# Moving 16 prompt tokens of a product-key layer from row fetches to dense products

## The chip, the cores and the metric

The kernel runs on one core of a Trainium2 chip. Its engines work beside one another and meet at semaphores: TensorE (PE in the profile), VectorE (DVE), ScalarE (ACT), GpSimd (POOL) and SyncE (SP), which issues most of the DMA transfers. The transfers of the core are carried by 16 DMA engines. The metric is the device time of one execution in microseconds (us), the median of several runs.

## The reference: what is computed

One decoder layer over 512 prompt tokens and 64 sample tokens (8 requests of 8), 2048 channels wide, all in float32: a modulated norm, a mixer with two kinds of heads, a residual; then a second modulated norm, the product-key retrieval ("PEER") that this change is about, a second residual and a final norm. The retrieval, per token and for each of 8 heads, picks 16 of 128 x 128 = 16384 experts, each one row of `peer_u` and one of `peer_v`:

```python
s1, i1 = lax.top_k(s[:, :, 0], PEER_TOPK)
s2, i2 = lax.top_k(s[:, :, 1], PEER_TOPK)
...
idx = jnp.take_along_axis(cidx, pos, axis=-1)
gates = jax.nn.softmax(top_s, axis=-1)
u_rows = p['peer_u'][idx]
act = jax.nn.gelu(jnp.einsum('phkd,pd->phk', u_rows, xb).astype(jnp.float32))
coef = (gates * act).astype(xb.dtype)
return jnp.einsum('phk,phkd->pd', coef, p['peer_v'][idx])
```

So a token needs 128 rows of `peer_u` and 128 rows of `peer_v`, 8 KB each. Both tables together hold 268 MB.

## The kernel before

The 576 tokens (T) lie along the free axis; the 2048 channels are 16 tiles of 128 partitions. For the retrieval they are parted in two.

**The dense tokens** (DT = 320: 256 prompt and 64 sample) are multiplied with all 16384 experts. The tables stream through once in "halves" of 128 x 1024 elements (512 KB): SP loads a half into `raw` (`load_half`, L233; four buffers in this stage, so a load waits until the half four before it has been split), ACT rounds it to `whi` (L244), POOL, or DVE for every fourth half, takes the rest `wlo` (L248, L253), and PE multiplies with three matmuls per tile (hi x hi, hi x lo, lo x hi), 24 matmuls of 320 columns for a half. A group is 4 x 128 experts: step A makes its `u` products (8 halves, L263), ACT applies gelu, DVE multiplies with the gates (L2195) and splits into `chi` and `clo`; step B makes the `v` products (8 halves, L2099) into two banks that DVE adds to `outacc` (L2228). There are 32 groups. The `u` products of the first two are made early, while DVE still selects the experts of the last head. Then 15 turns B, A, B, A follow (a turn is 32 halves, 768 matmuls), and two B at the end. The gates of a dense token, zero for nearly all experts, are built before that as outer products of one-hot rows (L1853 to L1902): 4 blocks of GB = 40 tokens to a loop turn, 8 tokens (an "octet") at a time, copied to `gst` and stored to `gateD` in HBM in pieces of 4 x 40 x 4 = 640 bytes, one store per block (L1831), two `gst` buffers.

**The sparse tokens** (SPT = 256, two row tiles of 128, one token on a partition) fetch only their own rows. `fetch` (L1801) is an indirect DMA of POOL: for one of the 128 slots it brings one row of 8 KB to each partition of a ring buffer, 1 MB. DVE takes a row set (`take`, L2162): for `u` a multiply and sum over 2048 elements, for `v` a multiply and add into PSUM. There are 512 fetches in this order: `u` of tile 0, `u` of tile 1, `v` of tile 0, `v` of tile 1, 128 each. The orders of POOL and DVE are written out in full for the whole stage: in the first eight turns 32 row sets fall to a turn (`rows_due`), in the seven later ones 35.4 on average, and 8 to the first B at the end. The ring has RING = 6 buffers; a fetch into one waits until DVE has taken what was in it. `xrow` holds the token rows of tile 1 until ACT copies them to PSUM between the two tiles of `u` (`between_rows`, L2142).

The query product (L1607, `parted`) multiplies with columns 0:256 and 256:576, one from each layout (`hi_s`, `hi_d`).

## Time and profile before

| | us |
|---|---|
| median of 3 runs | 4236.36 (4228.61 to 4244.34) |
| the profiled execution | 4242.22 |
| its span, first to last instruction | 4240.3 |

| engine | busy us | share of the span |
|---|---|---|
| PE | 3691.2 | 87% |
| DVE | 3024.4 | 71% |
| POOL | 2050.7 | 48% |
| ACT | 1471.0 | 35% |
| 16 DMA engines (mean) | 1090.68 MB moved | 257 GB/s over the span |

The program runs in stages. Modulation, mixer and output projection take the time up to about 1690 us, query and selection up to 2007 us with the early products in their last 65 us, the building of the gates 2007 to 2152 us. The stage of dense products and row sets runs from 2160 to 4216 us, nearly half of the span, and the final norm and output close it. A mean over the span mixes these: TensorE is the busiest engine on the page, while the DMA engines, with 257 GB/s on average, carry about 400 GB/s in the last stage. So the stage is read by itself, in stretches of one turn.

### The profile page before, as it was taken

What the parts mean: (1) busy time and instruction counts of PE and PEld (TensorE: products, weight loads), DVE (VectorE), ACT (ScalarE), POOL (GpSimd) and SP (SyncE); (2) the same over time, 40 slices, a digit from 0 to 9 for tenths busy, and PEclk for the clock granted to TensorE, in tenths of its full rate; (3) what the DMA queues carried; (4) which work ended last, traced back from release to release, by engine and by line L of the source; (5) the groups of instructions that cost most, each with busy time, mean ns of one, the idle gap of its engine ahead of it and who ended that gap; (6) DMA issues with size and microseconds to landing.
All of it is one profiled execution on the core that took longest, in us unless ns stands there. A gap on an engine that the chain in (4) does not pass through costs nothing. (4 is left out here: it accounts for less than half of the span.)

```text
span 4240.3 us, 66262 instructions
## 1 busy us (share of the span) xinstructions
PE 3691.2 (87%) x24298; PEld 3423.3 (81%) x24298; DVE 3024.4 (71%) x4791; ACT 1471.0 (35%) x1882; POOL 2050.7 (48%) x1144
## 2 busy tenths in 40 slices
PE   6876999999997898997679999999999898898986
PEld 3335988888896797997578888999898888888886
DVE  4777655566655214898978777778878888888886
ACT  5665444434442113222332332333332322223222
POOL 2333222222224233334047676777777767676772
PEclk9997999999998898998999999999999999999998
DMA  7991222222222123222589999999999999999994
GB/s 301 347 345 66 87 81 85 75 81 79 75 66 100 53 101 114 74 78 92 174 317 401 397 415 396 402 408 418 414 401 405 412 396 418 403 409 416 406 413 169
DMA packets 256208, 1090.68 MB, mean 257 GB/s; under 512 B 25352, under 2 KB 78856, under 8 KB 176392
## 3 DMA queue, kind: packets, MB, share of 16 engines
q1 hardware_dynamic: 170512, 543.60, 34.6%
q0 software_dynamic: 73728, 536.90, 30.9%
q10 hardware_dynamic: 11776, 7.52, 0.6%
q8 instruction: 132, 2.16, 0.2%
q14 instruction: 60, 0.49, 0.0%
HBM read 1047.54 MB, written 40.40 MB: 257 GB/s over the span
## 5 line engine op out<-in xcount | busy, mean ns | idle before, releaser
L248 POOL TENSOR_TENSOR wlo<-raw,whi 128x1024 fp32r<-128x1024 f32 x551 | 1344.4, 2443 | 1333.5 <-ACT whi L244 1328.2
L244 ACT CAST whi<-raw 128x1024 fp32r<-128x1024 f32 x670 | 699.1, 1049 | 1285.2 <-DMA raw<-in_u 535.1
L2099 PE MATMUL gps<-chi,whi 128*128 128x320 f32 x2048 | 656.7, 321 | 110.5 <-DVE outacc L2228 80.9
L263 PE MATMUL gps<-hi_d,whi 128*128 128x320 f32 x2048 | 653.2, 319 | 92.7 <-DVE wlo L253 61.9
L2099 PE MATMUL gps<-chi,wlo 128*128 128x320 f32 x2048 | 645.8, 315 | 0.0
L2099 PE MATMUL gps<-clo,whi 128*128 128x320 f32 x2048 | 645.7, 315 | 0.0
L263 PE MATMUL gps<-lo_d,whi 128*128 128x320 f32 x2048 | 643.6, 314 | 0.0
L263 PE MATMUL gps<-hi_d,wlo 128*128 128x320 f32 x2048 | 643.2, 314 | 0.0
L2186 DVE SCALAR_TENSOR_TENSOR dps<-ring,coef,dps 128x2048 f32<-128x2048 f32 x252 | 591.8, 2348 | 4.7 <-DVE dps L2186 0.9
L2173 DVE CUSTOM_DVE_ANT_0 ring<-ring,dps 128x2048 f32<-128x2048 f32 x256 | 582.2, 2279 | 0.0
L280 PE MATMUL gps<-act_hi,whi 128*128 128x288 f32 x2080 | 477.2, 311 | 37.9 <-POOL act_lo L511 9.0
L2099 PEld LDWEIGHTS gps<-chi,whi 128*128 128x128 f32 x2048 | 397.1, 194 | 130.9 <-DVE outacc L2228 92.8
L263 PEld LDWEIGHTS gps<-hi_d,whi 128*128 128x128 f32 x2048 | 394.4, 193 | 113.9 <-DVE wlo L253 69.8
L1807 POOL DMA_INDIRECT ring<-in_u_rows,spi x256 | 262.6, 1026 | 395.8 <-DVE udot L2173 224.9
L280 PE MATMUL gps<-act_hi,wlo 128*128 128x288 f32 x2080 | 450.1, 298 | 0.0
L280 PE MATMUL gps<-act_lo,whi 128*128 128x288 f32 x2080 | 448.4, 297 | 0.0
L2099 PEld LDWEIGHTS gps<-clo,whi 128*128 128x128 f32 x2048 | 397.2, 194 | 0.3
L2099 PEld LDWEIGHTS gps<-chi,wlo 128*128 128x128 f32 x2048 | 396.1, 193 | 0.0
L263 PEld LDWEIGHTS gps<-lo_d,whi 128*128 128x128 f32 x2048 | 394.4, 193 | 0.0
L263 PEld LDWEIGHTS gps<-hi_d,wlo 128*128 128x128 f32 x2048 | 394.4, 193 | 0.0
L280 PEld LDWEIGHTS gps<-act_hi,whi 128*128 128x128 f32 x2080 | 337.2, 192 | 63.5 <-issue 35.7
L280 PEld LDWEIGHTS gps<-act_hi,wlo 128*128 128x128 f32 x2080 | 338.3, 191 | 0.0
(384 smaller groups left out, 5906.6 us busy)
## 6 DMA issues: line engine op xcount, KB each, us to landing
raw<-in_u SPq DMA_DIRECT2D x256, 512.0 KB, 10.5
raw<-in_v SPq DMA_DIRECT2D x256, 512.0 KB, 8.6
wada<-in_w_ada SPq DMA_DIRECT2D x96, 1024.0 KB, 6.6
raw<-in_w_in SPq DMA_DIRECT2D x96, 512.0 KB, 3.4
gateD<-gst SPq DMA_DIRECT2D x8, 2560.0 KB, 9.9
gate<-gateD SPq DMA_DIRECT2D x32, 640.0 KB, 13.5
raw<-in_w_out SPq DMA_DIRECT2D x32, 512.0 KB, 3.7
raw<-in_w_q SPq DMA_DIRECT2D x32, 512.0 KB, 3.8
```

The source lines that it names most:

```text
L244: act.copy(whi[:, k.slot, :], raw_of(k)).then_inc(W.hi, 1)
L248: pool.tensor_tensor(wlo[:, k.slot, :], raw_of(k), whi[:, k.slot, :].bitcast(F32), ALU.subtract).then_inc(W.lo, 1)
L263: m = pe.matmul(gps[:, bank, 0:DT], w, x[:, kt, :], start=(kt == 0 and n == 0), stop=(kt == KT - 1 and n == 2))
L280: m = pe.matmul(gps[:, 2 * pair + th, 0:cols.stop - cols.start], w, parts[th][part][:, kt, cols], start=(kt == 0 and n == 0), stop=(kt == ...
L1807: pool.indirect_dma_start(out=rings[row_slot[n]][:, :], out_offset=None, in_=src, in_offset=bass.IndirectOffsetOnAxis(ap=spi[:, tile % NST ...
L2099: m = pe.matmul(gps[:, 2 + dt, 0:DT], w[:, slot, cols], x[:, buf, c, :], start=(c == 0 and n == 0), stop=(c == NG - 1 and n == 2))
L2173: m = dve.tensor_tensor_reduce(out=got, in0=got, in1=rows4, scale=1.0, scalar=0.0, op0=ALU.mult, op1=ALU.add, accum_out=udot[:, tile, j:j ...
L2186: m = dve.scalar_tensor_tensor(got if j == NSLOT - 1 else rows4, got, by, rows4, ALU.mult, ALU.add)
```

## The change

The split moves from 256 and 320 tokens to 240 and 336. The first row tile keeps 128 tokens, the second has 112: its fetches, multiplies and final transposes use partitions 0 to 111. All dense products of the retrieval have 336 columns. The gates are built in 3 loop turns of 4 blocks of 28 tokens in place of 2 turns of 4 blocks of 40: 42 octets and 12 stores in pieces of 4 x 28 x 4 = 448 bytes. The sparse layout `hi_s` stays 256 columns wide, so tokens 240 to 255 stand in both layouts and the query product still multiplies 256 and 320 columns. The larger dense buffers leave no room for the sixth ring buffer: its place is taken by `xrow`, which is free only after ACT has copied it, so the ring has five buffers up to row set 132 and six from 133. `udot` is cleared once, since tile 1 no longer fills all partitions.

```diff
-SPT = 256
-NST = SPT // P
+SPT = 240
+NST = 2
+SW = NST * P
+SROWS = (P, SPT - P)
 DT = T - SPT
-GB = 40
+GB = 28
...
-        hi_s, lo_s = (sb(n, [P, KT, SPT], F32R, at=at2nd) for n in ("hi_s", "lo_s"))
+        hi_s, lo_s = (sb(n, [P, KT, SW], F32R, at=at2nd) for n in ("hi_s", "lo_s"))
...
-        parted = [(hi_s, lo_s, slice(0, SPT)), (hi_d, lo_d, slice(0, DT))]
+        parted = [(hi_s, lo_s, slice(0, SW)), (hi_d, lo_d, slice(SW - SPT, DT))]
...
+        XROW_FROM = NSLOT + RING - 1
...
-                free[0:0] = range(RING0, RING)
+                free[0:0] = range(RING0, RING - 1)
+            if n == XROW_FROM:
+                free[0:0] = [RING - 1]
...
+            elif n == XROW_FROM:
+                pool.wait_ge(xrow_free, 1)
             tile, j = n // NSLOT, n % NSLOT
             src = a["u_rows"] if tile < NST else a["v_rows"]
+            used = slice(0, SROWS[tile % NST])
             pool.indirect_dma_start(
-                out=rings[row_slot[n]][:, :], out_offset=None, in_=src,
-                in_offset=bass.IndirectOffsetOnAxis(ap=spi[:, tile % NST, j:j + 1], axis=0)
+                out=rings[row_slot[n]][used, :], out_offset=None, in_=src,
+                in_offset=bass.IndirectOffsetOnAxis(ap=spi[used, tile % NST, j:j + 1], axis=0)
             ).then_inc(w_row[row_slot[n]], 16)
...
-        rings += [sb(f"ring{n}", [P, D], at=at7) for n in range(RING0, RING)]
+        rings += [sb(f"ring{n}", [P, D], at=at7) for n in range(RING0, RING - 1)] + [xrow]
...
-                    fetched, due = [RING0], [RING0 - RING]
+                    fetched, due = [RING0], [RING0 + 1 - RING]
...
-                        if n < min(due[0] + RING - (LAG if n >= NSP // 2 else 0), NSP):
-                            fetch(pool, n, S.taken)
+                        if n < min(due[0] + RING - (n < XROW_FROM) - (LAG if n >= NSP // 2 else 0), NSP):
+                            fetch(pool, n, S.taken, S.xt)
...
+                    ch(dve.memset(udot[:, :, :], 0.0))
```

On POOL, where tile 0 of the `u` rows gives way to tile 1 (the number in a ring's name is its buffer; `raw_11280` and `raw_10635` are the same load buffer). Before:

```order
352 L1807 DMA ring_8956<-in_u_rows,spi 128x2048
353 L248 TENSOR_TENSOR wlo<-raw_11280,whi 128x1024
354 L1807 DMA ring_8957<-in_u_rows,spi 128x2048
355 L248 TENSOR_TENSOR wlo<-raw,whi 128x1024
356 L1807 DMA ring_8958<-in_u_rows,spi 128x2048
357 L1807 DMA ring_8959<-in_u_rows,spi 128x2048
358 L248 TENSOR_TENSOR wlo<-raw_11280,whi 128x1024
359 L1807 DMA ring_11281<-in_u_rows,spi 128x2048
360 L248 TENSOR_TENSOR wlo<-raw_11280,whi 128x1024
361 L1807 DMA ring_11282<-in_u_rows,spi 128x2048
```

The same place on POOL after the change:

```order
355 L1816 DMA ring_8958<-in_u_rows,spi 128x2048
356 L1816 DMA ring_8959<-in_u_rows,spi 112x2048
357 L251 TENSOR_TENSOR wlo<-raw_10635,whi 128x1024
358 L1816 DMA ring_10636<-in_u_rows,spi 112x2048
359 L251 TENSOR_TENSOR wlo<-raw_10635,whi 128x1024
360 L1816 DMA ring_8956<-in_u_rows,spi 112x2048
361 L251 TENSOR_TENSOR wlo<-raw,whi 128x1024
362 L1816 DMA ring_8957<-in_u_rows,spi 112x2048
363 L1816 DMA ring_8958<-in_u_rows,spi 112x2048
364 L251 TENSOR_TENSOR wlo<-raw_10635,whi 128x1024
365 L1816 DMA xrow<-in_u_rows,spi 112x2048
```

A fetch stands at the same point between the `wlo` of the halves; it is one row set less ahead, it brings 112 rows from tile 1 on, and the first one into `xrow` has a `wlo` between it and the fetch before.

On DVE, at the end of a step A and the start of a step B around the first take of tile 1. Before (each take is the row with a ring in it and the short one behind it):

```order
1645 L2173 ISA ring_11282,udot<-ring_11282,dps 128x2048
1646 L2173 ISA udot 128x1
1647 L2200 TENSOR_TENSOR clo<-gps,chi 128x320
1648 L253 TENSOR_TENSOR wlo<-raw,whi 128x1024
1649 L2228 TENSOR_TENSOR outacc<-outacc,gps 128x320 x2
1650 L2173 ISA ring_8956,udot<-ring_8956,dps 128x2048
```

After:

```order
1640 L2185 ISA ring_8958,udot<-ring_8958,dps 128x2048
1641 L2185 ISA udot 128x1
1642 L2212 TENSOR_TENSOR clo<-gps,chi 128x336
1643 L256 TENSOR_TENSOR wlo<-raw,whi 128x1024
1644 L2240 TENSOR_TENSOR outacc<-outacc,gps 128x336 x2
1645 L2185 ISA ring_8959,udot<-ring_8959,dps 112x2048
```

Nothing changes places on DVE; the dense instructions are 16 elements longer, and a take of tile 1 has 112 partitions and the same 2048 elements on each.

## Rows read from the trace of the kernel before

**Rows 1.** The page: the GB/s of 40 slices, and two DMA issues.

```profile
GB/s 301 347 345 66 87 81 85 75 81 79 75 66 100 53 101 114 74 78 92 174 317 401 397 415 396 402 408 418 414 401 405 412 396 418 403 409 416 406 413 169
...
gateD<-gst SPq DMA_DIRECT2D x8, 2560.0 KB, 9.9
```

**Rows 2.** Windows of one turn each: stretch, length, busy us per engine, clock, DMA share, GB/s.

```profile
core 0: us, PE busy (x) PEld busy (x) DVE busy (x) ACT busy (x) POOL busy (x), PEclk, DMA share, GB/s
2160.20:2289.15 128.95, 117.78 (x769) 114.42 (x769) 102.52 (x128) 42.50 (x53) 91.31 (x56) 0.98 1.01 405
2289.15:2419.29 130.14, 119.22 (x768) 116.83 (x769) 100.34 (x120) 40.79 (x49) 89.71 (x56) 0.96 0.99 399
...
2802.44:2926.46 124.02, 115.74 (x769) 112.63 (x769) 100.33 (x120) 39.82 (x48) 91.05 (x56) 1.00 1.01 413
2926.46:3051.13 124.67, 116.05 (x770) 112.67 (x769) 100.34 (x120) 39.82 (x48) 90.94 (x56) 1.00 1.02 414
...
3718.07:3851.53 133.46, 119.07 (x771) 116.89 (x769) 114.84 (x92) 39.69 (x48) 94.25 (x60) 0.96 1.01 410
3851.53:3985.21 133.68, 120.67 (x770) 119.09 (x769) 115.26 (x92) 39.37 (x48) 95.20 (x60) 0.94 1.00 407
3985.21:4121.12 135.91, 119.60 (x770) 117.24 (x769) 114.95 (x92) 39.38 (x48) 94.82 (x60) 0.96 1.01 414
```

**Rows 3.** DMA view, 2700 to 3180 us: row queue (packets, MB, share), two issues.

```profile
q0 software_dynamic: 17493, 127.43, 64.6%
...
raw<-in_v SPq DMA_DIRECT2D x61, 512.0 KB, 8.4
...
ring<-in_u_rows,spi POOLq DMA_INDIRECT x117, 9.0
```

**Rows 4.** What PE waited for, 2300 to 4100 us: total, times, longest.

```profile
PE gps L2099 <- DVE outacc L2228: 74.7, 58, 3.7
PE gps L263 <- DVE wlo L253: 55.5, 27, 3.7
PE gps L263 <- POOL wlo L248: 27.5, 29, 2.9
PE gps L2099 <- DVE clo L2200: 3.9, 1, 3.9
```

**Rows 5.** What ACT waited for, the same stretch.

```profile
ACT whi L244 <- DMA raw<-in_u: 480.7, 163, 7.5
ACT whi L244 <- DMA raw<-in_v: 331.5, 132, 8.7
```

**Rows 6.** The DMA view of 1931 to 1938 us: loads with little beside them.

```profile
raw<-in_u SPq DMA_DIRECT2D x2, 512.0 KB, 3.4
```

**Rows 7.** Timeline of PE, from 1759.8 us (columns 320 and 256).

```profile
1759.83 0.31 PE L280 MATMUL gps<-lo_d,whi 128*128 128x320 f32 x1
1759.98 0.28 PE L280 MATMUL gps<-hi_s,wlo 128*128 128x256 f32 x1
1760.10 0.31 PE L280 MATMUL gps<-hi_d,wlo 128*128 128x320 f32 x1
```

**Rows 8.** Timeline of PE in a step B: start, duration.

```profile
2871.74 0.31 PE L2099 MATMUL gps<-chi,whi 128*128 128x320 f32 x1
...
2872.77 0.31 PE L2099 MATMUL gps<-clo,whi 128*128 128x320 f32 x1
```

**Rows 9.** Timeline of DVE in the building of the gates: two octets.

```profile
2126.66 1.21 DVE L1878 TENSOR_TENSOR gb<-pairT,const 128x1024 f32<-128x1024 f32 x1
...
2129.84 1.21 DVE L1878 TENSOR_TENSOR gb<-pairT,const 128x1024 f32<-128x1024 f32 x1
```

**Rows 10.** DMA view, 2031 to 2041 us: one gate store (pieces of 640 bytes).

```profile
q1 hardware_dynamic: 4112, 2.62, 85.0%
```

**Rows 11.** DMA view, 469 to 476 us: a store in pieces of 432 bytes.

```profile
q10 hardware_dynamic: 144, 0.06, 3.0%
```

**Rows 12.** DMA view, 401 to 404 us: a store from 8 partitions, 9216 bytes each.

```profile
q1 hardware_dynamic: 16, 0.07, 20.9%
...
rowsD<-rowT SPq DMA_DIRECT2D x1, 72.0 KB
```

**Rows 13.** DMA view, 4228.5 to 4239.5 us: stores of the output from 128 partitions.

```profile
q1 hardware_dynamic: 1025, 4.13, 94.0%
```

**Rows 14.** The row fetches (L1807): time from issue to landing.

```profile
DMA to landing us min/median/max: 5.4/9.4/14.1
```

**Rows 15.** Timeline of ACT: the copy of `xrow` between the tiles.

```profile
2678.32 1.87 ACT L2142 COPY dps<-xrow 128x2048 f32<-128x2048 f32 x1 [1.77 <-DVE udot L2173]
```

More of the change, by code:

```diff
@@ L1376, in build @@
         X.saved, = sems(stack, "x_saved")
-        at4 = [after]
+        at4 = [after2]
         x1T = sb("x1T", [P, KT, T], at=at4)
@@ L1497, in build @@
         EARLY = 2
-        at5 = [after]
+        at5 = [after2]
         clo = sb("clo", [P, EARLY, NG, DT], F32R, at=at5)
-        early = sb("early", [P, EARLY, NG, DT], at=[after])
+        early = sb("early", [P, EARLY, NG, DT], at=[after2])
         spi = sb("spi", [P, NST, H * TOPK], U32, at=at5)
@@ L1656, in body @@
                                 act.wait_ge(S.score, h * 2 + (s - 1))
-                            ch(act.copy(qt[:, s, 0:SPT], gps[:, 2 * s, 0:SPT]))
-                            act.copy(qt[:, s, SPT:T], gps[:, 2 * s + 1, 0:DT]).then_inc(S.qev, 1)
+                            ch(act.copy(qt[:, s, 0:SW], gps[:, 2 * s, 0:SW]))
+                            act.copy(qt[:, s, SW:T], gps[:, 2 * s + 1, 0:T - SW]).then_inc(S.qev, 1)
                             if s == 0 and later:
@@ L1799, in build, with fetch @@
             used_last[slot] = n
-        def fetch(pool, n, taken):
+        def fetch(pool, n, taken, xrow_free=None):
             if row_before[n] is not None:
                 pool.wait_ge(taken, row_before[n] + 1)
+            elif n == XROW_FROM:
+                pool.wait_ge(xrow_free, 1)
             tile, j = n // NSLOT, n % NSLOT
             src = a["u_rows"] if tile < NST else a["v_rows"]
+            used = slice(0, SROWS[tile % NST])
             pool.indirect_dma_start(
-                out=rings[row_slot[n]][:, :], out_offset=None, in_=src,
-                in_offset=bass.IndirectOffsetOnAxis(ap=spi[:, tile % NST, j:j + 1], axis=0)
+                out=rings[row_slot[n]][used, :], out_offset=None, in_=src,
+                in_offset=bass.IndirectOffsetOnAxis(ap=spi[used, tile % NST, j:j + 1], axis=0)
             ).then_inc(w_row[row_slot[n]], 16)
@@ L1839, in _ @@
                     for k in range(3):
-                        for t in range(NCH - NST):
-                            pe.transpose(gps[:, k, t * CH:(t + 1) * CH], slots[:, NST + t, k, :], ident)
+                        for t in range(NCH - NST + 1):
+                            pe.transpose(gps[:, k, t * CH:(t + 1) * CH], slots[:, NST - 1 + t, k, :], ident)
                         m = pe.transpose(gps[:, 3, k * TS:(k + 1) * TS], slots[0:TS, NCH, k, :], const[0:TS, 0:TS])
@@ L1862, in _ @@
                     for k in range(3):
-                        act.copy(slotT[k][:, 0:DT - TS], gps[:, k, 0:DT - TS]).then_inc(S.trev, 1)
+                        act.copy(slotT[k][:, 0:DT - TS], gps[:, k, SROWS[1]:SROWS[1] + DT - TS]).then_inc(S.trev, 1)
                         act.copy(slotT[k][:, DT - TS:DT], gps[:, 3, k * TS:(k + 1) * TS]).then_inc(S.trev, 1)
@@ L2058, in B @@
                             next_row()
-                    for _ in range(RING - RING0):
+                    for _ in range(RING - 1 - RING0):
                         next_row()
@@ L2072, in from_rows @@
                             for t in range(NST):
[L2073 to L2075 removed]
+                                o, n_ = (k % 8) * SW + t * P, SROWS[t]
+                                m = pe.transpose(rows4[:, o:o + n_],
+                                                 rings[row_slot[(LAST0, NSP - 1)[t]]][0:n_, k * P:(k + 1) * P],
+                                                 ident[0:n_, 0:n_])
                         m.then_inc(S.tr, 1)
@@ L2167, in take @@
                         tile, j = n // NSLOT, n % NSLOT
-                        got = rings[row_slot[n]][:, :]
+                        used = slice(0, SROWS[tile % NST])
+                        got, acc = rings[row_slot[n]][used, :], rows4[used, :]
                         dve.wait_ge(w_row[row_slot[n]], 16 * row_turn[n])
@@ L2172, in take @@
                                 dve.wait_ge(S.xt, tile)
-                            m = dve.tensor_tensor_reduce(out=got, in0=got, in1=rows4, scale=1.0, scalar=0.0,
+                            m = dve.tensor_tensor_reduce(out=got, in0=got, in1=acc, scale=1.0, scalar=0.0,
                                                          op0=ALU.mult, op1=ALU.add,
-                                                         accum_out=udot[:, tile, j:j + 1])
+                                                         accum_out=udot[used, tile, j:j + 1])
                         else:
```

14 lines of the change are left out of this document (6 added, 8 removed).

## The prediction, made before the changed kernel ran

> **What bounds the kernel now.** I read the GB/s line of the page first: over the last half of the span it stands at about 400, over the middle below 120 [rows 1]. The change acts mostly there, so I took windows of one turn (32 halves, 768 matmuls) [rows 2]. Three things are to be seen. The DMA share is 0.99 to 1.02 in every turn: the 16 engines are never idle. PE is busy 116 to 121 us of 124 to 136, and 13 of those us are only the modelled ends: eight consecutive starts take 1.03 us, 147 ns each [rows 8], so 768 matmuls need 112.9 us. And the turn's length follows the row sets: 32 of them in the first eight turns, 124.0 to 130.1 us; 35.4 in the later ones, 133.5 to 135.9 us in the rows shown, with the same matmuls in both.
>
> In bytes: a turn loads 32 x 0.524 = 16.8 MB of halves, 4 x 0.655 = 2.6 MB of gates and 32 x 1.049 = 33.6 MB of rows, 53.0 MB, later 56.5 MB. The ratio is 1.067; 134.4 us (mean of the three later turns) over 127 us (about the mean of the first eight, of which two ends are shown) is 1.06. That is a stage bound by DMA. The waits agree: ACT waits 812 us for halves to land, 480.7 + 331.5 [rows 5]; a half takes 8.4 us from issue to landing there [rows 3] and 3.4 us with little beside it [rows 6]. PE waits 162 us of 1800, for `outacc`, `wlo` and `clo` [rows 4], which come late because of that or because DVE is inside a take. DVE never waits for a row set: its ring is full in time.
>
> **Outside that stage** there is no DMA to hide behind. (1) Early products: 8 x 48 = 384 matmuls, back to back. Sixteen columns more cost 16/320 of 147 ns, 7.3 ns; the step from 256 to 320 columns (0.12 to 0.14 us between starts [rows 7]) gives 5 to 7 ns. I take 7: +2.7 us. (2) Gates: DVE makes an octet in 3.18 us (2126.66 to 2129.84 [rows 9]) and sets the pace; two more octets are +6.4 us. The stage ends when the last store has landed, now 9.9 us [rows 1]. A store keeps 4112 packets; a 640-byte one takes 0.85 x 10 us x 16 / 4112 = 33 ns [rows 10], a 432-byte one 0.03 x 7 x 16 / 144 = 23 ns [rows 11]. At 25 ns the last store lands about 2 us earlier: -2 us. The other stores end beside the building: a block of 28 tokens takes 3.5 x 3.18 = 11.1 us. (3) The two B at the end: 384 matmuls, +2.7 us. (4) 16 columns more in the second modulation and one memset: +0.5 us. Sum: **+10.3 us**.
>
> **The turns, PE side.** 768 x 7.3 ns = 5.6 us of PE per turn, 84 us over 15 turns. While DMA sets the turn this lies in PE's idle time: 127 - 112.9 = 14 us early, 134.4 - 112.9 = 21 us later, less what the half clock takes (clock 0.94 to 1.00). It isn't free: PE has less room after a late half. The bounds are 0 and 5.6 us a turn. I take 1 us, nearer to nothing, because the later turns took 3.5 MB more at the same rate, 407 to 414 GB/s, with PE at a different load: **+15 us**. DVE's 752 dense instructions get 16 elements longer, about 17 ns by 482 ns for 320 and its fixed part: 12 us in all, in the same shade.
>
> **The turns, DMA side.** Tile 1's 256 fetches bring 112 rows: 33.6 MB less. The row queue spends 0.646 x 480 x 16 = 4961 engine-us on 127.43 MB [rows 3], 319 ns for a row of 8 KB with its share of the small packets, so a fetch holds each of 16 engines for 8 x 319 ns = 2.55 us. Spread evenly, 112 rows would hold them 7 x 319 ns: 0.32 us less, 82 us over 256 fetches. That is one bound. The other is above nothing, and here I chose against the bytes. The trace has one transfer that doesn't cover 128 partitions and is large enough to read: the store of `rowT` from 8 partitions. Its 8 packets of 9216 bytes take 0.209 x 3 us x 16 = 10.0 engine-us, 1.25 us each [rows 12], 7.4 GB/s per engine. Stores from 128 partitions run at 4.13 MB / (0.94 x 11 us x 16) = 25 GB/s [rows 13]. So an engine's rate depends on which partitions the transfer touches: neighbours share something that 128 partitions use evenly. In a fetch of partitions 0 to 111 the sixteen missing rows are neighbours too. If they lie on a few of these shared ways, the others carry as much as before, and the fetch holds the transfers as long as one of 128 rows. I take that: **0 us** for tile 1's bytes, the value between the bounds that the nearest row speaks for.
>
> The Trainium skill, page "SBUF — State Buffer", section "Door 1: The DMA port swizzle", says this in full: 16 ports of 8 partitions, by bits of the partition number, about 27 GB/s each. By it partitions 112 to 127 share four ports with 80 to 95, so twelve ports keep their eight rows a fetch; the sum stays at 0 for this term, where bytes alone would give -82 us before PE's floor. The trace agrees in the one place it can: four neighbours on one port would be a quarter of the rate, and 7.4 of 25 is 0.30.
>
> **Ring and new wait.** With five buffers a fetch is issued at least four takes ahead, 4 x 3.9 us = 15.6 us, and lands in 9.4, at most 14.1 us [rows 14]: hidden, at about 0. The fetch into `xrow` waits on POOL for ACT's copy of 1.87 us, which starts when tile 0's last `u` row is taken [rows 15]. Queued behind it are POOL's `wlo` halves, for which PE waits. But the fetch before it waits for the same take and a `wlo` of 2.4 us stands between: 0, at worst 2 us, once.
>
> **Sum.** 10.3 + 15 + 0 = +25 us. Against the profiled execution 4242.2 + 25 = 4267; against the median, 6 us below it, 4236 + 26: **4262 us**, 0.6% slower.
>
> **Rivals.**
> A. *Bytes count evenly; faster or no change.* For it: DMA is the bound, and 4.2 MB of 53.0 go in a tile-1 turn. Against: rows 12. The gain stops at the next floor. Early tile-1 turns: DMA 125 x 48.9/53.0 = 115 us, PE 118.5 us plus about 3.5 for the change of step where DVE is late, so 123.5 in place of 125: -1.5 x 4. Later ones: DMA 124 us, DVE 116 + 1, PE 118.5 + 3.5 + 3 for the clock, so 128 in place of 134.4: -6.4 x 3.6 = -23. Tile 0 keeps +1 x 7.6. Total 10.3 + 7.6 - 29 = -11: 4225 us, 4200 to 4245. It decides when a tile-1 row packet stays near 319 ns.
> B. *The 112 rows get in one another's way; slower.* If the even split gives an engine seven rows that lie on other engines' ways, packets slow down. 8/7 x 319 = 365 ns is the point at which nothing is saved; at 400 ns a fetch costs 7 x 35 = 0.25 us more, +63 us over 256. With the 25: 4325 us. The far end, 1.25 us as in rows 12, would be over 1000 us; I don't hold the range to it, since there only 8 partitions were in use. For it: the same rows. Against: in 112 rows the neighbours need not coincide.
> C. *PE becomes the bound everywhere*: 5.6 x 15 + 10.3 = +94, 4330 us. For it: the half clock in some turns. Against: the idle time above.
> D. *Pieces of 448 bytes are slow.* The Trainium skill, page "DMA: Bandwidth & Descriptors", section "Specifications", wants at least 512 bytes and names a read-modify-write below. From rows: were a packet twice the 33 ns, a store would take 17 us against 11.1 us of building, and 12 of them 204 us in place of 140: +64 and the 25, 4325 us. The 23 ns of rows 11 speak against it.
>
> **How the numbers follow.** Forecast 0.40, A 0.30, B 0.23, C 0.04, D 0.03. The forecast's own range is 4245 to 4280. The range for 8 in 10 runs from inside A, 4210, to inside B, 4345. The measurement tells about 0.5% (21 us) from no change. Faster by more: a quarter of A, 0.08. Within: most of A, 0.20, 0.17 of the forecast and 0.02 of B, 0.39. Slower: the rest, 0.53.
>
> **What the changed profile would show.** PE starts 154 ns apart, and no PE wait in the early products. Gates: 42 octets, stores landing in about 8 us; 13 or more means D. Turns of tile 0: 1 us longer, DMA share still 1.0. Turns of tile 1: the same length as before with fewer GB/s (about 380 in place of 410) if I am right; share below 1 and turns of 124 and 128 us for A; row packets over 365 ns and longer turns for B. A DVE wait for a ring buffer would make the five-buffer step wrong; a `wlo` wait beside the first fetch into `xrow`, the new wait. The forecast is wrong if DMA isn't the bound of tile 0's turns, or if tile 1's lose length.

## The result: 9.8% slower

| | before | after |
|---|---|---|
| median of 4 runs, us | 4237.92 | 4659.50 (4618.67 to 4684.12) |
| ratio, 95% interval | 1 | 1.0982 [1.0940, 1.1023] |
| the profiled execution, us | 4242.22 | 4676.66 |
| its span, us | 4240.3 | 4674.7 |

The forecast was 4262, its range 4210 to 4345: the time lies 315 us above the range. The GB/s line of the page after, beside [rows 1], shows where. The 40 slices are now 117 us each.

```profile
GB/s 302 354 272 74 85 76 82 77 69 82 65 85 82 101 95 74 75 168 268 386 382 405 379 246 275 299 282 281 280 401 404 400 413 298 265 261 258 249 262 152
...
L2198 DVE SCALAR_TENSOR_TENSOR dps<-ring,coef,dps 128x2048 f32<-128x2048 f32 (+1 forms) x205 | 481.8, 2350 | 77.8 <-DMA ring<-in_v_rows,spi 75.0
...
gateD<-gst SPq DMA_DIRECT2D x12, 1792.0 KB, 8.8
```

Twice the rate falls from about 400 to 250 to 300 GB/s, in six slices and then in six more: these are tile 1 of `u` and tile 1 of `v`, the two quarters whose fetches bring 112 rows. Between them stands tile 0 of `v`, with 128 rows a fetch, at 400 and more. And DVE waits 75.0 us for row sets of `v`, which it never did before.

The windows of one turn each, as in [rows 2] (stretch, length, busy us of PE, PEld, DVE, ACT, POOL, clock, DMA share, GB/s). The first two are of tile 0 of `u`, then two of tile 1 of `u`, one of tile 0 of `v`, two of tile 1 of `v`:

```profile
2166.42:2297.76 131.34, 122.94 (x769) 120.68 (x769) 103.68 (x128) 43.87 (x54) 88.38 (x56) 0.98 0.98 392
2297.76:2431.90 134.14, 123.35 (x769) 120.74 (x769) 101.19 (x121) 39.01 (x47) 88.73 (x57) 0.97 0.97 385
...
2697.49:2882.79 185.30, 136.74 (x771) 131.53 (x769) 104.31 (x120) 41.24 (x49) 89.73 (x58) 0.88 1.02 259
2882.79:3051.13 168.34, 134.04 (x770) 130.56 (x769) 104.12 (x120) 40.22 (x49) 89.06 (x56) 0.89 1.02 292
...
3388.97:3525.65 136.68, 125.10 (x770) 122.87 (x769) 116.98 (x93) 39.55 (x49) 94.94 (x60) 0.96 1.00 403
...
4139.60:4335.88 196.28, 138.08 (x769) 131.99 (x769) 114.47 (x92) 39.65 (x48) 91.74 (x60) 0.87 1.01 257
4335.88:4535.32 199.44, 137.45 (x768) 131.64 (x769) 113.84 (x93) 39.65 (x48) 91.06 (x59) 0.86 1.01 256
```

A turn of tile 1 takes 166 to 199 us in place of 124 to 136, with fewer bytes, the DMA share still at 1.01 or 1.02 and the busy time of DVE, ACT and POOL little changed. The granted clock falls to 0.86 to 0.91, a mean of 1.2 and 2.4 GHz: in 2880 to 3060 us there are seven stretches of 3.4 to 10.2 us at the lower level, each soon after PE had stood idle for 1.8 to 8.7 us. So the DMA engines are full and move less. The DMA view tells why (queue: packets, MB, share of the 16 engines; then issues with KB and median us to landing). First 2700 to 3380 us, tile 1 of `u`:

```profile
q0 software_dynamic: 16170, 115.88, 63.9%
...
raw<-in_u SPq DMA_DIRECT2D x64, 512.0 KB, 16.8
...
ring<-in_u_rows,spi POOLq DMA_INDIRECT x103, 13.9
```

Then 3950 to 4550 us, tile 1 of `v`:

```profile
q0 software_dynamic: 14015, 100.44, 66.2%
...
raw<-in_u SPq DMA_DIRECT2D x48, 512.0 KB, 21.1
...
ring<-in_v_rows,spi POOLq DMA_INDIRECT x87, 19.5
```

The working of [rows 3]: 0.639 x 680 x 16 = 6952 engine-us for 115.88 MB is 491 ns for a row of 8 KB; in the second stretch it is 518 ns. Before it was 319. A load of `in_u` lands after 16.8 and 21.1 us, before after 11.0 and 10.1 (2700 to 3180 and 3500 to 4100 us). In the recorded packets the row packets of tile 1 have a mean of 486 (`u`) and 513 ns (`v`), in tile 0 325 and 318; the packets of the loads beside them (4 KB) 232 and 245 ns in place of 163 to 167.

What waited in 3900 to 4580 us (us in total, times, longest):

```profile
POOL wlo L251 <- ACT whi L247: 302.9, 73, 14.7
ACT whi L247 <- DMA raw<-in_u: 243.6, 44, 12.1
ACT whi L247 <- DMA raw<-in_v: 231.7, 53, 5.7
DVE gps L2207 <- ACT gps L2131: 111.9, 22, 11.4
...
PE gps L266 <- POOL wlo L251: 83.4, 20, 10.4
```

A late half is late for ACT, then for POOL's `wlo`, then for PE. ACT's longest wait for a load is 12.1 us, before it was 8.7 [rows 5]; PE's longest is 10.4 us, before it was 3.9 [rows 4].

### The profile page after: what moved, and what is told of

Its sections match the earlier page's. It is cut to its first block and busy times, and to the rows that moved or that the text cites. A ratio compares the mean times of both kernels' runs of the same rounds, so it can differ in the third digit from the quotient of the medians.

```text
span 4674.7 us, 66414 instructions
## 1 busy us (share of the span) xinstructions
PE 3872.3 (83%) x24333; PEld 3592.8 (77%) x24333; DVE 3055.5 (65%) x4810; ACT 1473.8 (32%) x1886; POOL 2019.2 (43%) x1144
## 5 line engine op out<-in xcount | busy, mean ns | idle before, releaser
L2109 PE MATMUL gps<-chi,whi 128*128 128x336 f32 x2048 | 692.1, 338 | 227.3 <-DVE outacc L2240 147.8
L266 PE MATMUL gps<-hi_d,whi 128*128 128x336 f32 x2048 | 680.5, 332 | 232.8 <-POOL wlo L251 156.7
L2109 PE MATMUL gps<-clo,whi 128*128 128x336 f32 x2048 | 677.4, 331 | 7.1 <-issue 7.1
L2109 PE MATMUL gps<-chi,wlo 128*128 128x336 f32 x2048 | 677.4, 331 | 0.0
L266 PE MATMUL gps<-lo_d,whi 128*128 128x336 f32 x2048 | 668.6, 326 | 0.0
L266 PE MATMUL gps<-hi_d,wlo 128*128 128x336 f32 x2048 | 667.9, 326 | 0.0
L2185 DVE CUSTOM_DVE_ANT_0 ring<-ring,dps 128x2048 f32<-128x2048 f32 (+1 forms) x235 | 534.8, 2280 | 0.0
L2198 DVE SCALAR_TENSOR_TENSOR dps<-ring,coef,dps 128x2048 f32<-128x2048 f32 (+1 forms) x205 | 481.8, 2350 | 77.8 <-DMA ring<-in_v_rows,spi 75.0
L1816 POOL DMA_INDIRECT ring<-in_u_rows,spi x235 | 225.2, 958 | 342.8 <-DVE udot L2185 168.5
L2240 DVE TENSOR_TENSOR outacc<-outacc,gps 128x336 f32<-128x336 f32 x512 | 251.7, 500 | 178.9 <-PE gps L2109 177.7
## 6 DMA issues: line engine op xcount, KB each, us to landing
gate<-gateD SPq DMA_DIRECT2D x32, 672.0 KB, 16.8
```

The source lines that it names most:

```text
L266: m = pe.matmul(gps[:, bank, 0:DT], w, x[:, kt, :], start=(kt == 0 and n == 0), stop=(kt == KT - 1 and n == 2))
L1816: pool.indirect_dma_start(out=rings[row_slot[n]][used, :], out_offset=None, in_=src, in_offset=bass.IndirectOffsetOnAxis(ap=spi[used, tile ...
L2109: m = pe.matmul(gps[:, 2 + dt, 0:DT], w[:, slot, cols], x[:, buf, c, :], start=(c == 0 and n == 0), stop=(c == NG - 1 and n == 2))
L2185: m = dve.tensor_tensor_reduce(out=got, in0=got, in1=acc, scale=1.0, scalar=0.0, op0=ALU.mult, op1=ALU.add, accum_out=udot[used, tile, j:j ...
L2198: m = dve.scalar_tensor_tensor(got if j == NSLOT - 1 else acc, got, by, acc, ALU.mult, ALU.add)
L2240: dve.tensor_tensor(out, out, gps[:, 2 + dt, 0:DT], ALU.add).then_inc(S.acc, 1)
```

## The experiments

All kernels are compared with the kernel before on the same chip. Where the time went is read by turns: the sum of the turns of each quarter, from the windows of the profiled executions, in us (the twelfth turn, in the third column, already has some row sets of tile 1 of `v`).

```
kernel           stage starts   u tile 0 u tile 1 v tile 0 v tile 1  rest    span
                                (4)      (4)      (4)      (3)
before                2160.2    514.9    500.2    542.8    403.0    119.2  4240.3
after                 2166.4    531.1    691.5    559.4    586.9    139.4  4674.7
before_fetch112       2160.1    513.6    704.0    549.6    583.8    145.5  4656.6
after_fetch128        2164.6    536.6    537.4    546.4    411.5    119.2  4315.8
skip_last16           2163.8    512.9    501.9    534.0    401.8    119.2  4233.6
skip_every8           2157.4    514.6    501.5    541.8    403.0    118.8  4237.0
before_ring5          2153.7    516.5    519.3    538.6    403.4    118.9  4250.5
ring5_catchup         2159.2    519.1    501.4    534.6    400.4    118.4  4233.0
cols336               2159.8    517.3    508.2    544.1    402.7    120.5  4252.6
ring5_cols336         2157.6    523.6    530.0    535.7    405.8    119.4  4272.1
after128_cols320      2160.7    526.1    517.7    535.5    402.7    118.4  4261.1
gates_once            2158.9    498.9    486.6    534.1    396.6    118.3  4193.5
after_skip_every8     2160.7    531.6    537.5    545.8    412.0    118.8  4306.4
before_cols304        2161.0    513.6    503.6    530.0    402.5    118.1  4228.8
before_lag0           2159.0    516.0    500.2    539.7    501.3    116.7  4332.8
before_lag1           2163.6    515.6    500.2    531.0    397.4    121.4  4229.1
before_lag01          2157.6    518.2    501.1    525.3    399.5    121.6  4223.3
```

Each line is one execution, and the quarters that an edit doesn't touch show how far they wander: tile 0 of `u` between 512.9 and 518.2, tile 1 of `u` within 1 us of 500.2, tile 0 of `v` from 534.0 to 542.8. Smaller differences in one column say nothing.

### The shape of the fetch, in the kernel

The theory after the result: a fetch of 112 partitions slows the packets of the rows and of all that runs beside them. The rival: the loss comes from the ring, the longer products or how they act together. The kernel before, with nothing changed but the 112 rows in tile 1 (its last 16 tokens get no rows, and their token rows are zero):

```diff
+            used = slice(0, 112 if tile % NST else P)
-                out=rings[row_slot[n]][:, :], out_offset=None, in_=src,
-                in_offset=bass.IndirectOffsetOnAxis(ap=spi[:, tile % NST, j:j + 1], axis=0)
+                out=rings[row_slot[n]][used, :], out_offset=None, in_=src,
+                in_offset=bass.IndirectOffsetOnAxis(ap=spi[used, tile % NST, j:j + 1], axis=0)
```

> The kernel before with one edit: tile 1's fetches bring 112 rows (16 tokens are left out: their token rows are zeroed, the instruction counts and sizes of all engines stay). Theory P: tile 1's turns lengthen by 45 and 60 us as in the changed kernel, about 4237 + 390 = 4630 us. Rival Q: 4237 or less.

And the changed kernel with 128 rows in tile 1 again (`used = slice(0, P)`):

> The changed kernel, but tile 1 fetches all 128 rows again (DVE still uses 112 of them). Theory P: the row packets return to 320 ns, tile 1's turns to about 130 and 136 us, and what is left over the kernel before is the 336 columns, the gates and the five-buffer ring: 4265 to 4285 us. Rival Q (336 columns, 112-partition DVE work or the ring cause the loss): it stays within 100 us of 4660.

before_fetch112: 4653.06 us (two runs), ratio 1.0969 [1.0936, 1.1001]. after_fetch128: 4318.91 us, 1.0179 [1.0157, 1.0202], 34 us above the range expected for it. The 112 rows make nearly the whole loss by themselves, 416 us, and giving the 16 rows back to the changed kernel wins 341. The two parts, 416 and 82, are more than the 422 together; that fits DMA as the bound of tile 1, beside which the other part has room again, but no run shows it by itself. One turn of tile 1 of `u` in each, in this order:

```profile
2855.08:3030.72 175.64, 132.10 (x769) 126.49 (x769) 101.15 (x120) 39.76 (x48) 87.06 (x56) 0.88 1.02 273
```

```profile
2965.42:3102.00 136.58, 126.31 (x770) 124.67 (x769) 106.41 (x120) 39.72 (x48) 91.67 (x57) 0.95 0.95 378
```

### The shape alone

A kernel of nothing but transfers: sections of 20 fetches of 8 KB rows to 128, 120, 112, 96 and 64 partitions, then with 20 loads of 512 KB beside them, then 40 loads alone. Nothing of the layer is computed, the outputs are zeros.

```diff
+                            pool.indirect_dma_start(
+                                out=rings[slot][0:width, :], out_offset=None, in_=a["u_rows"],
+                                in_offset=bass.IndirectOffsetOnAxis(ap=idx[0:width, n % NIDX:n % NIDX + 1], axis=0)
+                            ).then_inc(s_row[slot], 16)
```

> A kernel that computes nothing of the layer (its outputs are zeros): sections of 20 row fetches each, up to five in flight, to partitions 0:128, 0:120, 0:112, 0:96 and 0:64 alone, then 20 fetches of 128, 112 and 96 partitions beside 20 loads of 512 KB, then 40 loads alone. Theory P (neighbouring partitions share a way into SBUF, and a fetch of fewer than 128 rows sends several engines down the same way): 128 rows run at about 26 GB/s per engine (320 ns a row), 112 rows alone have packets clearly over 365 ns, so a fetch of 112 takes longer than one of 128, 96 as well, and 64 rows (half of the ways) about as long as 128. Beside loads, 112-row fetches stretch the loads' 4 KB packets from 160 to over 220 ns too. Rival Q (the slow packets come from this kernel's other traffic or timing, not from the shape of the fetch): 112 rows alone take 7/8 of the time of 128, at about 320 ns a row.

A single run, 732 us. Its windows by section (stretch, length, POOL busy, clock, DMA share, GB/s): 128, 120, 112, 96, 64 partitions, then 128 with loads, 112 with loads, and loads alone:

```profile
2.92:57.32 54.40, 18.89 (x20) 1.00 0.94 386
58.26:150.87 92.61, 19.45 (x20) 1.00 0.97 212
151.77:219.96 68.19, 18.30 (x20) 1.00 0.97 269
220.85:287.73 66.88, 18.07 (x20) 1.00 0.96 235
288.62:341.59 52.97, 17.85 (x20) 1.00 0.96 198
341.67:419.48 77.81, 18.69 (x20) 1.00 0.99 404
419.73:519.44 99.71, 18.35 (x20) 1.00 0.99 289
...
619.63:674.88 55.25, 0.00 (x0) 1.00 0.97 380
```

Share x length x 16 over the rows gives per row packet 320 ns for 128 partitions, 599 for 120, 472 for 112, 535 for 96 and 636 for 64. So 112 rows take 68.2 us where 128 take 54.4, and no width in between is cheaper than 128; 120 is the worst. With the loads, the mix of the kernel's turn, a pair of fetch and load takes 4.99 us in place of 3.89. A turn of 32 pairs is then 160 us, and 124.5 with 128 rows: the kernel has 166 to 185, and 124 to 127. The shape alone makes most of the loss, with no engine computing. It isn't POOL's share of the work either: a fetch holds POOL for 0.9 to 1.0 us at every width (18.89 / 20 for 128 partitions, 18.30 / 20 for 112).

Two more readings bear on how the rows are dealt to the engines. In the prediction's picture twelve engines keep eight rows and four have four, so that the share could reach at most (12 x 8 + 4 x 4) / 128 = 0.88 of full; it is 0.97 with 112 partitions, so the work is spread over all 16. And the DMA view counts 320 packets of 4 bytes beside the rows of 20 fetches, 16 a fetch, at every width but 120: there it counts 480, 24 a fetch, so the worst width is cut up in another way.

The Trainium skill, page "SBUF — State Buffer", section "Door 1: The DMA port swizzle", says that 64 partitions reach half of the ports and about half of the rate; 198 against 386 GB/s agrees. One way to it is rival B's: 16 engines carry a fetch, and if 112 rows are dealt out seven to an engine in order, one engine's rows lie on several of those ports and several engines meet at one. Which rows an engine carries no record here shows, so this is argued, not shown.

### Fewer bytes in the old shape

If that is so, a fetch that keeps 128 partitions but skips 16 rows, leaving each engine on its own way, must not slow down. The rival says that any missing row upsets it. The index of the skipped partitions is put out of bounds, and the 16 tokens are left out: partitions 112 to 127 in skip_last16, every eighth one (7, 15, ...) in skip_every8.

```diff
+                    ch(dve.tensor_scalar(slots[:, 1, 0, :], slots[:, 1, 0, :], const[:, C_SKIP:C_SKIP + 1], None, ALU.add))
+            more = dict(bounds_check=NKEY * NKEY - 1, oob_is_err=False) if tile % NST else {}
-                in_offset=bass.IndirectOffsetOnAxis(ap=spi[:, tile % NST, j:j + 1], axis=0)
+                in_offset=bass.IndirectOffsetOnAxis(ap=spi[:, tile % NST, j:j + 1], axis=0), **more
```

> The kernel before; tile 1's fetches keep all 128 partitions, but the indices of partitions 112 to 127 lie beyond the table's bound, so their rows are skipped (these 16 tokens are left out). The same bytes as with 112 rows. Theory P with the engines kept on their own ways: no packets slow down; the ways of the other rows carry as much as before, so 4230 to 4245 us, unchanged. If bytes were all that counts: 4200 or less. If skipping rows as such is slow: over 4300.

> The kernel before; tile 1's fetches keep 128 partitions but skip the rows of partitions 7, 15, ... 127 (16 tokens left out), so each group of neighbours loses one row in eight. The same bytes as skip_last16 and as 112 rows. Theory P with DMA as the bound of tile 1's turns: the whole saving is open, 0.32 us a fetch, 82 us at most; PE and DVE stop it: 4237 - 15 to - 45, so 4190 to 4222 us. If the stage is held equally by something else (PE's own idle time, DVE): within 10 us of 4237, as skip_last16.

The same in the changed kernel:

> The changed kernel with 128-partition fetches in tile 1 that skip every eighth row: 336 dense columns, the saved bytes taken evenly from all ways (other tokens left out than the kernel needs, the sizes are those of the change). It is what the change would have been had bytes counted evenly. Theory C (with 336 columns PE, not DMA, holds the early turns; after_fetch128 showed a DMA share of 0.95): little comes of it, 4290 to 4315 us. Rival A of the prediction (DMA is still the bound): 4225 to 4250 us.

skip_last16: 4240.35, 0.9998 [0.9983, 1.0012]. skip_every8: 4240.72, 1.0008 [0.9995, 1.0021]. after_skip_every8: 4313.95, 1.0178 [1.0156, 1.0199], the same as after_fetch128. A turn of tile 1 of `u` in skip_last16 and in skip_every8:

```profile
2801.59:2925.74 124.15, 116.98 (x768) 112.64 (x769) 101.15 (x121) 40.08 (x48) 95.84 (x56) 1.00 0.98 382
```

```profile
2798.05:2922.27 124.22, 117.33 (x768) 112.67 (x769) 101.16 (x121) 40.09 (x48) 95.86 (x56) 1.00 0.99 381
```

Row packets stay at 320 to 323 ns, so the shape and not the number of rows is the cause. skip_last16 says more: it brings the same rows to the same partitions, 0 to 111, as before_fetch112, and is 413 us faster. What differs is the width that the instruction states, and with it how the rows are dealt out.

The second finding was expected of skip_last16 and not of skip_every8, where 4190 to 4222 was the range if DMA is the bound: some 31 GB/s less, and the turn keeps its length within 0.2 us (124.02 in [rows 2]). In skip_last16 loads even land after 8.6 us in place of 11.1 (median of the `u` halves, 2700 to 3150 us). Fewer row bytes, taken in this way, win nothing.

But the edit takes away less than its bytes. In 2700 to 3150 us the row queue's share falls from 0.651 to 0.578 and 0.582, while the plain loads need 0.393 and 0.403 for the 65 MB that took 0.362; about half of the saving is gone. And a fetch with the bounds check holds POOL for 1.17 us in place of 1.01, 5 us more in a turn. So these two runs are not DMA alone made lighter.

### What else holds the turn

Three runs take something else away or add to it. 16 columns less in the dense products (the last 16 dense tokens get no products):

```diff
-                                gemm_dense(pe, k.plus(2 * c + half), half, c % 2)
+                                gemm_dense(pe, k.plus(2 * c + half), half, c % 2, DT - 16)
```

> The kernel before with 16 columns fewer, 304, in all dense matmuls of the last stage (the last 16 sample tokens' products are left out; DVE and ACT work on 320 as before). PE needs 15 x 768 x 7.5 ns = 86 us less. If DMA alone holds the turns: 4225 to 4240 us. If PE's columns count in full on the path: 4150 us. Theory C says PE and DMA are nearly level in the kernel before, so down to DMA's floor only: about 4215 to 4235 us.

16 columns more in 15 of 16 matmuls of A and 3 of 4 of B (`DT + 16` there; these columns hold neighbours' data, and their products are used by nothing):

> The kernel before; the matmuls of the last stage take 16 more columns (the neighbours' first columns, into bank columns that nobody reads), except those of the last tile of a product, so about 0.84 of the change's extra PE time, 5 us a turn; everything else as before. The step lengths so far: a step B holds DVE 0.93 to 0.98 busy and went from 30.6 to 33.3 us in after_fetch128, a step A stayed. Theory C: steps B lengthen by 1.5 to 2.5 us, A by under 0.5: 4237 + 40 to 65 us. The prediction's term (PE's columns lie in idle time, 1 us a turn): 4237 + 8 to 20.

And the gates of the first two groups used by all, with 30 loads of gates left out:

```diff
-                            if j == 0:
-                                load_gates(g, buf)
-                        dve.wait_ge(s_gate[g % 2], g // 2 * 16 + 16)
+                        dve.wait_ge(s_gate[g % 2], 16)
```

> The kernel before without the 30 later gate loads (all groups use the gates of the first two; 20 MB less). Steps A take 32 to 33.7 us where PE needs 28.1; skipping row bytes left them as they were. Theory G (a step A is held by the halves queued behind the gate load on SP's queue): steps A lose 1.5 to 3 us each, 4237 - 45 to - 90. If A is held by DVE and POOL: within 15 us of 4237.

before_cols304: 4229.09, 0.9973 [0.9963, 0.9982]: 11 us won for 86 us of PE, a time that lies in two of the three expected ranges. cols336: 4246.76, 1.0017 [0.9999, 1.0035]: 8 us lost for 71 us, not clear of the noise, and as the prediction's term has it. gates_once, a little less than the 45 us expected: 4197.23, 0.9904 [0.9884, 0.9923]. A turn of tile 1 of `u` there:

```profile
2900.68:3022.02 121.34, 115.36 (x769) 112.65 (x769) 100.32 (x120) 40.27 (x48) 91.02 (x56) 1.00 1.02 415
```

30 loads of 640 KB, 20 MB or 2.5% of the stage's bytes, bring 41 us, 2% of the stage's time, while 256 x 16 rows, 34 MB or 4%, bring nothing. ACT's longest wait for a `u` half in 2700 to 3150 us falls from 6.8 to 2.7 us (in the skip runs it stays at 7.2 and 7.4), and the steps A, from first matmul to first matmul, shrink from 33.7 to 31.5 us (tile 0) and 32.0 to 30.3 (tile 1), the steps B not at all. So a step A is held by its load of gates. Whether by the halves that queue behind it or by the bytes as such is open: in tile 1 of `u` a step A moves 13.2 MB in 32.0 us with the gates and 12.6 in 30.3 without, 414 and 416 GB/s, which is what a bound by DMA would give, and for the steps A only the skip runs speak against it.

A step B of tile 1 of `u` takes 30.55 us on average in the kernel before, with the DMA at 387 or at 418 GB/s, and as long in gates_once; in skip_last16 and skip_every8 it is 30.8. With 16 columns less it takes 29.7 and with the columns of cols336 31.2; with DVE's slow `wlo` of before_ring5, below, 32.7 (means of eight steps). DVE is busy 27.4 us of it, 0.90, not the 0.93 to 0.98 of the expectation for cols336. So DVE and PE hold a step B together. Two such steps of the kernel before, in the order of the windows above:

```profile
2675.06:2705.58 30.52, 28.84 (x193) 28.26 (x193) 27.39 (x36) 10.88 (x11) 23.12 (x15) 1.00 0.99 387
2864.23:2894.77 30.54, 28.78 (x193) 28.25 (x193) 27.41 (x36) 9.27 (x10) 22.48 (x15) 1.00 1.02 418
```

In before_cols304 the steps A of tile 1 give back what the steps B win, 33.3 us in place of 32.0. The turn has several limits of nearly the same length: taking away from one brings little.

### The ring of five

The kernel before with five buffers up to row set 132 and then six, its columns and fetches as they were:

```diff
-                free[0:0] = range(RING0, RING)
+                free[0:0] = range(RING0, RING - 1)
+            if n == FULL_FROM:
+                free[0:0] = [RING - 1]
-                        if n < min(due[0] + RING - (LAG if n >= NSP // 2 else 0), NSP):
+                        if n < min(due[0] + RING - (n < FULL_FROM) - (LAG if n >= NSP // 2 else 0), NSP):
```

> The kernel before with five ring buffers up to row set 132 and six after it, nothing else. after_fetch128 is 82 us over the kernel before, and its tile-0 turns are 5 us longer. Theory C (the columns do it): 4237 within 8 us. Rival R (fetches come later, or POOL's waits move against the wlo halves): 4250 to 4280 us.

With one extra fetch at set 133, so that from there on the fetches are six ahead again:

```diff
+                            if n == FULL_FROM:
+                                fetch(pool, n + 1, S.taken)
+                                fetched[0] += 1
```

> before_ring5 with one fetch more at the point where the sixth buffer becomes free, so that from there on POOL is again six ahead and waits for DVE's latest take. Its loss of 14 us lies in the turns of tile 1 of u, where DVE's wlo rose from 1.22 us. Theory L (POOL out of step with DVE): those turns return from 129.8 to 125 us, 4237 within 6 us. Otherwise it stays at 4250 to 4256.

before_ring5: 4253.48, 1.0033 [1.0021, 1.0045]. ring5_catchup: 4241.41, 1.0009 [0.9994, 1.0023]. The 14 us lie in tile 1 of `u` (500.2 to 519.3), where the ring has six buffers again; in tile 0, with five, a turn is as before. No row set is late. The order keeps fetching five ahead there, one buffer is mostly free, and POOL no longer waits for DVE's take before each fetch. DVE's `wlo` in 2802 to 3175 us (count | busy us, mean ns | idle), before and then in before_ring5 and ring5_catchup:

```profile
L253 DVE TENSOR_TENSOR wlo<-raw,whi 128x1024 fp32r<-128x1024 f32 x24 | 29.4, 1225 | 0.0
```

```profile
L253 DVE TENSOR_TENSOR wlo<-raw,whi 128x1024 fp32r<-128x1024 f32 x24 | 44.3, 1844 | 0.0
```

```profile
L253 DVE TENSOR_TENSOR wlo<-raw,whi 128x1024 fp32r<-128x1024 f32 x24 | 29.4, 1224 | 0.0
```

The mean of the same instruction is 1.84 us in place of 1.22, and one more fetch undoes it. The mean hides two kinds: in before_ring5 12 of the 24 take 1.22 us and 12 take 2.42 to 2.61. Each of the slow ones starts while a `wlo` of POOL is running and ends 1.1 us after that one's end; none of the quick ones overlaps it by more than 0.31 us. One of each kind, with POOL's instruction above (start, duration):

```profile
2932.79 2.37 POOL L248 TENSOR_TENSOR wlo<-raw,whi 128x1024 fp32r<-128x1024 f32 x1 [2.44 <-ACT whi L244]
2933.66 2.59 DVE L253 TENSOR_TENSOR wlo<-raw,whi 128x1024 fp32r<-128x1024 f32 x1
...
2949.70 1.22 DVE L253 TENSOR_TENSOR wlo<-raw,whi 128x1024 fp32r<-128x1024 f32 x1
```

While POOL waits at each fetch, its own `wlo` fall at fixed points between DVE's; let loose, they meet. The Trainium skill, page "SBUF — State Buffer", section "Who interferes with whom", says that a DVE instruction with two SBUF inputs, as this one, contends with a GpSimd instruction that reads SBUF; the 2.42 to 2.61 us agree.

Then the kernel before has the same loss in its `v` half: LAG = 2 there makes it fetch four ahead with six buffers, five in the last quarter. LAG = 0 and LAG = 1 for the whole half, and, third, 0 for tile 0 and 1 for tile 1, so that the lead equals the buffers in both:

```diff
-                        if n < min(due[0] + RING - (LAG if n >= NSP // 2 else 0), NSP):
+                        if n < min(due[0] + RING - (LAG - 1 if n >= 3 * NSP // 4 else 0), NSP):
```

> The kernel before with LAG = 0 in place of 2: in the v half of the stage POOL issues a fetch as soon as DVE has freed the buffer, as in the u half, and so runs in step with DVE. Theory L (DVE's wlo takes 1.86 us there and 1.22 us in the u half because POOL's own work runs across it; POOL in step with DVE avoids that): the wlo returns to 1.22 us, turns 8 to 14 lose 2 to 5 us each, 4205 to 4225 us. Otherwise: POOL's waits delay its own wlo halves and the turns lengthen, 4240 to 4280 us.

> LAG = 1: between the two. Theory L: DVE's wlo between 1.22 and 1.86 us in turns 8 to 14, 4220 to 4235 us.

> The kernel before with LAG 0 for tile 0 of v (where before_lag0 took a turn from 134.6 to 130.6 us) and 1 for tile 1 of v, where the ring has lost the buffer that keeps tile 0's sum and LAG 0 made POOL wait (167 us a turn). Theory L: 4217 to 4227 us, below before_lag1's 4231.

before_lag0: 4340.04, 1.0242 [1.0215, 1.0270], far above both ranges expected; its turns of tile 0 of `v` take 130 to 131 us in place of 133 to 137, but those of tile 1, where the order is one ahead of the ring's five buffers, 163 to 172: POOL waits 165.0 us for DVE's takes in 3720 to 4100 us (51.6 before), and its `wlo` stand behind these fetches. before_lag1: 4230.60, 0.9970 [0.9959, 0.9981]. before_lag01: **4220.19, 0.9958 [0.9942, 0.9975]**, with all of the work in it, some 0.4% under the kernel before. A turn of tile 0 of `v` before and in before_lag01:

```profile
3309.25:3446.31 137.06, 120.22 (x770) 117.83 (x769) 115.15 (x91) 39.05 (x48) 95.36 (x60) 0.95 1.01 409
```

```profile
3307.34:3436.71 129.37, 116.29 (x770) 112.62 (x769) 108.97 (x91) 39.92 (x48) 93.81 (x59) 1.00 1.02 418
```

DVE's `wlo` in 3200 to 3650 us, in the same order:

```profile
L253 DVE TENSOR_TENSOR wlo<-raw,whi 128x1024 fp32r<-128x1024 f32 x26 | 49.7, 1911 | 0.0
```

```profile
L253 DVE TENSOR_TENSOR wlo<-raw,whi 128x1024 fp32r<-128x1024 f32 x27 | 34.3, 1269 | 0.0
```

### What remains in after_fetch128

It is 1.8% slower than before, some 80 us. Alone, ring (14) and columns (8 for 0.84 of them) make 22. Both together in the kernel before (the edits of before_ring5 and cols336):

> The kernel before with both edits that alone gave +14 us (five buffers up to row set 132) and +8 us (336 columns in most matmuls). after_fetch128 is +80, of which these and the longer gates explain some 28. Theory I (the two together cost more than one by one, because in steps B PE and DVE are level and each edit uses the other's room): 4237 + 40 to 70 us, steps B of the u half 33 us. Theory D (the rest comes from the longer DVE and ACT instructions): 4237 + 20 to 28.

And after_fetch128 with 320 columns in the dense products, all else of the change kept:

> after_fetch128 with the last stage's matmuls back at 320 columns (16 sample tokens' products left out); DVE and ACT still work on 336, the ring and the gates as in the change. PE needs 90 us less. Theory I: the interaction goes with the columns, 4255 to 4275 us, steps B of the u half back at 30.8 us. Theory D: 4290 to 4310 us.

ring5_cols336: 4274.17, 1.0083 [1.0066, 1.0101], 35 us, between the two ranges expected. after128_cols320: 4266.65, 1.0074 [1.0057, 1.0091], 31 us, inside the range of theory I; but its steps B take 32.3 and 32.6 us in the two tiles of `u` and not 30.8, so that theory's reason did not come out. By the ratios, the same columns cost 8 us alone, 21 beside the five-buffer ring, and some 45 on top of all the rest (1.0179 against 1.0074, with all of them). The parts don't add. Of the 31 us, 14 are the ring's; the table has what is left mostly in tile 0 of `u`, 526.1 us in place of 516.5 in before_ring5. What in "all the rest" makes it there (longer DVE and ACT instructions, larger loads of gates), and why columns weigh so much on top of it, was not taken apart and stays open.

## Why the prediction was wrong

**The step that failed is "The turns, DMA side".** It went from "an engine's rate depends on which partitions the transfer touches" to "the others carry as much as before", and took 0 us for the bytes of tile 1. The first half is right: with 64 partitions the rate is 198 GB/s, with 128 it is 386. The second assumed that 112 rows keep each engine on the way that it has with 128; that holds when 128 partitions are stated and 16 rows skipped, and not when 112 are stated. Rival B named the other case and its mechanism stands: row packets above 365 ns. Its size did not hold. The text put 400 ns, from no row, and said that the far end, 1.25 us [rows 12], was not to be held. Measured were 486 and 513 ns: 7 x (486 - 365) = 0.85 us a fetch of `u` and 7 x (513 - 365) = 1.04 of `v`, 241 us over 2 x 128. The second part was in no case at all: the loads beside the fetches slow down too, by 8 x (232 - 166) = 0.53 and 8 x (245 - 166) = 0.63 us a half, about 141 us over the 7.6 turns. Together 382 us; the table, from `u` tile 1 to the end, has 363 between after_fetch128 and after. The same sum with the packets of before_fetch112 (493 and 236 ns, 517 and 251) gives 401, where 416 were measured.

**"A stage bound by DMA" was not shown by what it rested on, and stays undecided for the kernel before.** The share of 1.0 and turns that grow with the row sets fit it, but a row set also costs 2.35 us of DVE, and so grows the turn without DMA. The steps B, equally long at 387 and at 418 GB/s, and the skip runs speak against it, the steps A of gates_once for it. In the changed kernel with 128 rows the share is 0.95, so there DMA isn't the bound of these turns; with the slow packets it is. Two readings under it were off: a turn loads gates twice and not four times (7 loads in 2700 to 3180 us), so it moves 51.7 MB and not 53.0, later 55.2, which leaves the ratio at 1.07. And of PE's 116 to 121 us not 13 but 3 to 8 are modelled ends, by the text's own 112.9.

**Rival A** (4225, chance 0.30) falls by its own condition, packets near 319 ns. In after_skip_every8, where an eighth fewer rows come at 329 ns a packet, the time is 4314, as in after_fetch128: even with quick packets no gain was there.

**The ring, "hidden, at about 0", was 14 us.** The lead of 15.6 us was enough: no row set came late. What was missed is that the length of the lead sets whether POOL and DVE run in step. The order of instructions could not show it, the times of DVE's `wlo` could.

**The columns.** 15 us for the turns, 12.6 for 0.84 of them; cols336 gives 8 by itself, with an interval from 0 to 15, so as an edit alone it was sized rightly. Added to the rest it was not: tile 0 of `u` lost 4.0 us a turn, not 1, of which 2.6 go with the columns (536.6 in after_fetch128, 526.1 in after128_cols320). The spacing was right: 154 ns, seven starts in 1.08 us (start, duration):

```profile
2999.74 0.32 PE L2109 MATMUL gps<-clo,whi 128*128 128x336 f32 x1
...
3000.82 0.32 PE L2109 MATMUL gps<-chi,wlo 128*128 128x336 f32 x1
```

**Outside the turns** nothing speaks against the sum, and little for it: the stage begins 6.2 us later than before, against 7.6 summed (early products, gates, modulation), but in kernels with no change ahead of the stage it begins anywhere from 2153.7 to 2163.6 us. The gate stores land after 8.8 us (median), against 9.9 less 2. Rival D falls: in 2020 to 2050 us, with two gate stores and little beside them, the row below gives 0.505 x 30 x 16 / 8224 = 29 ns a piece of 448 bytes, under the 33 of 640 bytes [rows 10].

```profile
q1 hardware_dynamic: 8224, 3.67, 50.5%
```

The first fetch into `xrow`, at 2709.1 us, waits for nothing: the new wait cost nothing. Rival C (PE everywhere) falls, with PE busy 0.7 to 0.8 of a tile-1 turn.

The direction came out, but by luck: the 25 us forecast came from columns and gates, and the 422 measured come nearly all from the term that was put at nothing. By size the forecast was off by a factor of 16, and the range's upper end was set by a number that no row gave.

## What to carry to other kernels

Keep an indirect fetch at all 128 partitions; to bring fewer rows, put their indices out of bounds, which here cost no time, and won none. When a transfer takes a shape that the trace has never shown, its far row belongs in the range, or the shape is timed alone first: twenty fetches would have said it. Before a resource is called the bound, take a little of it alone, and look what else the edit moved; a share of 1.0 and matching ratios are not enough. And where GpSimd and VectorE both read SBUF, look at the times of one VectorE instruction with two SBUF inputs: if some of them are twice as long as the others, change how far GpSimd runs ahead.

## What the hardware showed that was not expected

- Fetches of 8 KB rows, 20 of them: 54.4 us for 128 partitions, 92.6 for 120, 68.2 for 112, 66.9 for 96, 53.0 for 64. Half the rows take the time of all, and 120 rows 1.7 times that.
- A slow transfer slows its neighbours: 4 KB packets of plain loads to 128 partitions rose from 166 to 218 ns beside fetches of 112 rows with nothing else running, and to 232 to 245 in the kernel.
- Rows skipped by their index leave the other row packets at 320 to 323 ns; the plain loads beside them need about a tenth more engine time, and the fetch holds GpSimd 0.16 us longer.
- A DVE `tensor_tensor` with two SBUF inputs took 1.22 us between GpSimd's own and 2.42 to 2.61 us when it started inside one of them; in step with GpSimd its mean was 1.22 us, out of step 1.84 to 1.91.
